# A transformer layer with 32 routed experts on one core: the last expert pair written out for TensorE in both arms of the overflow question, loaded chunk by chunk, with its down product by column halves

## What is computed

```python
logits = (ht @ w_router + b_router)            # 32 experts
top_val, top_idx = lax.top_k(logits, 4)
gates = jax.nn.softmax(top_val, axis=-1)
...
hu = xb @ w_up[e] + b_up[e]                    # 1024 -> 2048
x_glu, x_lin = jnp.split(hu, 2, axis=-1)
x_glu = jnp.minimum(x_glu, 7.0)
x_lin = jnp.clip(x_lin, -7.0, 7.0)
act = x_glu * jax.nn.sigmoid(1.702 * x_glu) * (x_lin + 1.0)
y = act @ w_down[e] + b_down[e]                # 1024 -> 1024
return y * gate[:, None].astype(y.dtype)
```

## Time and profile before

| | |
|---|---|
| median of 3 runs | 1038.88 us |
| the profiled execution, device time | 1039.46 us |
| its span in the profile | 1037.2 us |
| PE busy | 1003.5 us, 97% |
| PE weight load busy | 389.4 us, 38% |
| DVE busy | 202.7 us, 20% |
| ACT busy | 114.7 us, 11% |
| DMA, mean of the span | 410 GB/s, 423.65 MB read |
| mean granted clock of TensorE | 0.995 |

### The profile page before, as it was taken

One profiled execution on the slowest core, in us unless ns is written; L12 is line 12 of the kernel. 1 busy time (PEld: TensorE's weight loads), 2 busy tenths in 40 slices (PEclk: granted clock), 3 DMA queues, 4 the chain that ended last, 5 costly groups with the idle time before them and its releaser, 6 DMA issues.

```text
span 1037.2 us, 10934 instructions
## 1 busy us (share of the span) xinstructions
PE 1003.5 (97%) x4494; PEld 389.4 (38%) x4494; DVE 202.7 (20%) x486; ACT 114.7 (11%) x230; POOL 12.8 (1%) x26
## 2 busy tenths in 40 slices
PE   8999999999999999999999999999998989999998
PEld 4446453434343433333333333332333324232432
DVE  0466132121121121212121211212011211112012
ACT  2426111010000001010101000100001000100000
POOL 0200000000000000000000000000000000000000
PEclk9999999999999999999999999999999999999999
DMA  9955979999999999999999999999999999999996
GB/s 369 382 239 232 395 294 427 432 438 412 426 434 431 430 435 431 430 433 431 432 432 431 431 435 430 433 432 430 433 432 428 435 431 428 435 431 427 432 428 262
DMA packets 22608, 424.94 MB, mean 410 GB/s; under 512 B 3616, under 2 KB 4384, under 8 KB 6720
## 3 DMA queue, kind: packets, MB, share of 16 engines
q1 hardware_dynamic: 22208, 424.17, 96.0%
q10 hardware_dynamic: 384, 0.54, 0.2%
HBM read 423.65 MB, written 1.05 MB: 409 GB/s over the span
## 4 chain that ended last, share of the span: by engine, by line
PE 70%; DMA 28%; another core or an unknown queue 1%; DVE 0%; issue 0%; ACT 0%; POOLq 0%; SPq 0%; POOL 0%; DVEq 0%
PE psum L1424 32%; DMA everything<-in_w_moe 27%; PE psum L1458 14%; PE psum L1090 4%; PE psum L1305 4%; PE psum L1344 4%; PE psum L1214 3%; PE psum L1057 3%; PE psum L1295 2%; PE psum L1065 2%; PE psum L1082 1%; PE psum L1073 1%; PE psum L1353 0%; DMA everything<-in_x_turned 0%; PE psum L1316 0%
## 5 line engine op out<-in xcount | busy, mean ns | idle before, releaser
L1424 PE MATMUL psum<-everything 128*64 128x512 f32 x2048 | 463.7, 597 | 2.0 <-DMA everything<-in_w_moe 1.8
L1458 PE MATMUL psum<-everything 128*64 128x512 f32 x1024 | 231.3, 602 | 21.0 <-DMA everything<-in_w_moe 20.9
L1424 PEld LDWEIGHTS psum<-everything 128*64 128x64 f32 x2048 | 137.9, 136 | 295.6 <-issue 286.4
L1458 PEld LDWEIGHTS psum<-everything 128*64 128x64 f32 x1024 | 73.3, 138 | 165.7 <-issue 151.3
L736 DVE TENSOR_TENSOR everything<-psum,everything 128x512 f32<-128x512 f32 (+1 forms) x38 | 25.0, 663 | 343.2 <-PE psum L1305 332.9
L1022 DVE TENSOR_SCALAR everything<-psum 128x512 f32<-128x512 f32 x32 | 22.1, 692 | 345.0 <-PE psum L1424 345.0
L1305 PEld LDWEIGHTS psum<-everything 128*128 128x128 f32 x480 | 55.8, 191 | 24.3 <-issue 24.3
L1344 PE MATMUL psum<-everything 128*128 128x512 f32 x128 | 64.2, 606 | 0.0
L693 ACT ACTIVATE everything<-everything 128x512 f32<-128x512 f32 x32 | 20.2, 631 | 388.7 <-DVE everything L1022 388.7
L1305 PE MATMUL psum<-everything 128*128 128x128 f32 x480 | 61.5, 281 | 0.0
L1090 PE MATMUL psum<-everything 128*128 128x512 f32 x96 | 42.1, 594 | 0.0
(11 more groups left out here) (160 smaller groups left out, 300.8 us busy)
## 6 DMA issues: line engine op xcount, KB each, us to landing
everything<-in_w_moe SPq DMA_DIRECT2D x80, 4096.0 KB, 43.4
everything<-in_w_moe SPq DMA_DIRECT2D x27, 2048.0 KB, 15.1
everything<-in_w_moe SPq DMA_DIRECT2D x8, 1024.0 KB, 8.8
everything<-in_w_in SPq DMA_DIRECT2D x3, 2048.0 KB, 25.6
everything<-in_w_out SPq DMA_DIRECT2D x2, 2048.0 KB, 10.4
everything<-in_w_mem_kv SPq DMA_DIRECT2D x1, 2048.0 KB, 17.1
everything<-in_w_moe SPq DMA_DIRECT2D x4, 512.0 KB, 36.6
everything<-in_w_in SPq DMA_DIRECT2D x1, 1024.0 KB, 8.2
```

The costliest lines, as they stand in the source:

```text
L1424: mm = pe.matmul(psum[r:r + SLOTS, bank], XT[:, k, r:r + SLOTS], weights[i][:, column:column + N], start=k == 0 and not first, stop=k == K ...
L1458: mm = pe.matmul(psum[r:r + SLOTS, DOWN_BANKS[n]], actT[:, 2 * i + k, r:r + SLOTS], slot[:, column:column + N], start=i == 0 and k == 0, s ...
```

## The change

- **The last pair on TensorE is no longer in the loop.** The loop runs pairs 2 to 14. After it TensorE reads the count and branches; pair 15 is written out in full in either arm. In the arm for overflow the further blocks follow it. The other arm stands behind both in the program.
- **The last pair's loads** are issued chunk by chunk from chunk 0 (two-chunk loads are gone there), and each odd chunk has a semaphore of its own (`odd_in`), which only the written-out pair waits for. In the loop an odd chunk is covered by the wait for the even one before it, and only chunk 11 has a wait (`eleventh_in`). The increments with which SyncE kept the old semaphores level (`credit`) are gone but for one.
- **The order in a down chunk** is `n` outside and `k` inside, for every pair, and the host lays the weights out so. Half 0 is complete after two of a chunk's four groups.
- **In the last pair** combines 0 and 1 stand between the third and the fourth group of chunk 11; ScalarE copies half 1 in two pieces of 256 columns, and combine 2 is two products of 256 columns, each behind its piece. Combine 3 ends the pair.
- ScalarE's last pair is written out behind its loop.

```diff
             def pair(q, p):
                 for d in range(TWOS):
                     wait_used(q, 2 * d + 1)
                     sp.dma_start(two_slots[d], two_chunks(p * TWOS + d)).then_inc(two_in[d], 16)
-                    credit(d)
+
+                sp.sem_inc(eleventh_in, 16)
...
             def last_pair():
                 q = PAIRS - 1
-                for d in range(2):
-                    wait_used(q, 2 * d + 1)
-                    sp.dma_start(two_slots[d], two_chunks(q * TWOS + d)).then_inc(two_in[d], 16)
...
+                for j in range(PAIR_CHUNKS):
+                    wait_used(q, j)
+                    src = chunk(q * PAIR_CHUNKS + j)
+                    if j == PAIR_CHUNKS - 2:
+                        arrived = two_in[j // 2], tenth_half_in
+                    elif j == PAIR_CHUNKS - 1:
+                        arrived = quarters_in
+                    else:
+                        arrived = (odd_in if j % 2 else two_in)[j // 2],
...
-                    nc.scalar.activation(Y[:, n * N:(n + 1) * N], psum[:, DOWN_BANKS[n]], ACT.Copy).then_inc(y_ready, 1)
+                    parts = ((0, N // 2, y_half), (N // 2, N, y_ready)) if last and n == 1 else ((0, N, y_ready),)
+                    for lo, hi, ready in parts:
+                        nc.scalar.activation(Y[:, n * N + lo:n * N + hi], psum[:, DOWN_BANKS[n], lo:hi], ACT.Copy
+                                             ).then_inc(ready, 1)
...
-                    for k in range(2):
-                        if not first and i == DOWN_CHUNKS - 2 and k == 1:
-                            pe.wait_ge(tenth_half_in, q * 16)
-                        for n in range(2):
-                            if not first and last:
-                                pe.wait_ge(quarters_in[2 * k + n], q * 16)
+                    for n in range(2):
+                        if last_pair and i == DOWN_CHUNKS - 2 and n == 1:
+                            pe.wait_ge(tenth_half_in, 16)
+                        for k in range(2):
+                            if last_pair and last:
+                                pe.wait_ge(quarters_in[2 * n + k], 16)
+                                if (n, k) == (1, 1):
+                                    combine(q, (0, 1))
                             for e in range(2):
...
                 if own:
                     combine(q)
+                elif last_pair:
+                    pe.wait_ge(y_half, 1)
+                    pe.matmul(psum[:, RESULT_BANKS[2], 0:N // 2], back[:, 0], Y[:, N:N + N // 2], start=False, stop=False,
+                              skip_group_check=True)
+                    pe.wait_ge(y_ready, 2 * q + 2)
+                    pe.matmul(psum[:, RESULT_BANKS[2], N // 2:N], back[:, 0], Y[:, N + N // 2:2 * N], start=False, stop=False,
+                              skip_group_check=True).then_inc(combined, 1)
+                    combine(q, (3,))
 
             pair(0, 0, first=True)
             pair(1, 1, second=True)
-            overflow = overflowing(pe)
-            with pe.Fori(2, PAIRS) as q:
+            with pe.Fori(2, PAIRS - 1) as q:
                 pair(q, q)
-            combine(PAIRS - 1)
-            with pe.If(overflow):
+            with pe.If(overflowing(pe)):
+                pair(PAIRS - 1, PAIRS - 1, last_pair=True)
                 further_blocks(pe, lambda r, p: pair(r + PAIRS, p, own=True))
+            with pe.Else():
+                pair(PAIRS - 1, PAIRS - 1, last_pair=True)
```

More of the change, by code:

```diff
@@ L467, in pair_before_last @@
                     sp.dma_start(two_slots[d], two_chunks(q * TWOS + d)).then_inc(two_in[d], 16)
[L468 to L469 removed]
+                for j, done in ((PAIR_CHUNKS - 2, two_in[TWOS - 1]), (PAIR_CHUNKS - 1, eleventh_in)):
                     wait_used(q, j)
                     sp.dma_start(slots[j], chunk(q * PAIR_CHUNKS + j)).then_inc(done, 16)
[L472 to L473 removed]
             def last_pair():
                 q = PAIRS - 1
[L477 to L488 removed]
+                for j in range(PAIR_CHUNKS):
[7 more added lines that the diff above has]
+                        arrived = (odd_in if j % 2 else two_in)[j // 2],
+                    size = SLOT_COLS // len(arrived)
+                    for k, done in enumerate(arrived):
+                        part = slice(k * size, (k + 1) * size)
+                        sp.dma_start(slots[j][:, part], src[:, part]).then_inc(done, 16)
             def store_result():
@@ L688, in _, with pair @@
                                  ).then_inc(gatesT_ready, 1)
-            def pair(q, bdown=False):
+            def pair(q, bdown=False, last=False):
                 for i in range(2):
@@ L1363, in turn_act, with wait_chunk @@
                 mm.then_inc(act_turned, 1)
-            def wait_chunk(q, j, first):
+            def wait_chunk(q, j, first, last, own):
                 if first:
@@ L1369, in wait_chunk, with pair @@
                         pe.wait_ge(two_in[j // 2], 32)
-                    return
-                arrived = (*(two_in[j // 2] if j % 2 == 0 else None for j in range(5)), fifth_in, two_in[3], seventh_in,
-                           two_in[4], ninth_in, two_in[5], None)[j]
-                if arrived is not None:
-                    pe.wait_ge(arrived, q * 16 + 16 * (TWO_LOADS[j // 2] - 1 if j % 2 == 0 else 0))
-            def pair(q, p, first=False, second=False, own=False):
+                elif j % 2 == 0:
+                    pe.wait_ge(two_in[j // 2], q * 16 + 16 * (TWO_LOADS[j // 2] - 1))
+                elif last and j < PAIR_CHUNKS - 1:
+                    pe.wait_ge(odd_in[j // 2], 16)
+                elif not last and not own and j == PAIR_CHUNKS - 1:
+                    pe.wait_ge(eleventh_in, q * 16)
+            def pair(q, p, first=False, second=False, own=False, last_pair=False):
                 half = UP_CHUNKS // 2
```

23 lines of the change are left out of this document (10 added, 13 removed).

## The result

The changed kernel takes **1041.14 us** (median of 20 runs, 1039.31 to 1044.03), the kernel before beside it on the same chip 1038.71 (20 runs, 1037.66 to 1039.60): ratio 1.0024, 95% interval 1.0018 to 1.0030. It is 2.4 us slower where 1.4 was forecast: inside the range, but on the other side of the 0.2% line, 2.1 us. The likeliest case was the wrong one of two near ones, and the next rival, the far jump that outlasts its cover, is what happened.

What follows compares the result with a forecast made beforehand. It took the weight stream to bound the loop and TensorE, 0.8 us behind, the end; tail +0.93, output -1.6 and branch +2.1 summed to +1.4 us, 1040.3 us on the median's footing, range 1037.8 to 1043.8.

Steps and rivals of the forecast that it cites:

- 0.2% line: Whole kernel: a difference within about 0.2%, 2.1 us, counts as no change; forecast inside it, chance 0.53.
- The likeliest case: Between pairs 14 and 15: as summed, branch of 4 to 6 us with the clock up, +1.4 us; chance 0.46.
- the far jump that outlasts its cover: Rival between pairs 14 and 15: branch of 6.0 us or more makes it slower, up to +5.7 us; chance 0.42.
- What bounds the kernel: Whole kernel: weight stream bounds the loop; TensorE, 0.8 us behind it, sets the end, so lost time isn't regained.
- The branch between the pairs: TensorE, pairs 14 to 15: far branch of 5.35 us, partly covered, puts chunk 0 at 980.0, +2.1 us.
- The clock: Behind TensorE's idling before pair 15: granted clock may drop to 1.2 GHz, +1.7 us; in the 0.42 rival, not the sum.
- with the clock, 4.3 us of branch would do: Slower rival, between pairs 14 and 15: if the clock also drops, a 4.3 us branch suffices, not 6.0; chance 0.42.
- Tail: End of pair 15: combines 0 and 1 moved ahead and half 1 copied in pieces delay VectorE's last sum, +0.93 us.
- Output: Last output tile: without an instruction packet beside it, it lands at the other tiles' pace, -1.6 us.
- Loads: Last pair: chunk 0 loaded alone lands one chunk earlier, removing TensorE's 0.18 us wait and no more.
- Loop: Loop pairs: changed semaphore increments, waits and product order gain nothing, since the stream is the bound there.
- The fetch rule: TensorE's branches: a taken branch to a target outside the two pages held forces an instruction fetch before execution goes on.

Runs made afterwards that it cites:

- question_after_pair_8: Changed kernel with TensorE's count question after pair 8, both arms holding a loop of pairs 9 to 14 and pair 15: 1038.30 us, 0.9993 of the kernel before.
- one_copy: Changed kernel with pair 15 written out once behind the loop, count read after pair 1, branch at the very end: 1037.95 us, 0.9989 of the kernel before.
- arms_swapped: Changed kernel with the question reversed, so the arm that is run stands right behind the branch: 1037.69 us, 0.9991 of the kernel before.
- question_after_pair_1: Changed kernel with the question after pair 1, both arms holding a loop of pairs 2 to 14 and pair 15: 1039.51 us, 1.0008 of the kernel before.

## Why the prediction was partly right

- **What bounds the kernel.** Right: nothing after the branch gave time back, and without the stall TensorE and the stream end close together: it waits 0.17 us for the last quarter in `question_after_pair_8`, and in `one_copy` it comes to combines 0 and 1 at 1026.99, 0.95 us behind the last weight.
- **The branch between the pairs.** This step failed. Its place, its cover (3.3 us, forecast 3.2) and its packet were right. "Branch 5.35 us, chunk 0 at 980.0, +2.1" was 6.48 us in the changed kernel, and 6.09 to 6.73 in the four kernels with the question there: the idling is 1.0 us more than the sum had. The bounds of 3.35 and 9.65 held it; the value in the lower third was chosen because the packet is one and that load was 32. But most of the time is not the packet's transfer (1.07 us): it begins 4.0 us after the branch where it began 1.0 after on idle engines. That the gather started at 977.28, where "late by about 2 us, at 977" was forecast, is luck: the branch began at 970.6, 1.0 us before its forecast, and took 1.1 longer.
- **The clock.** The second part of the miss, 1.6 us in the profiled execution. It stood in the rival, not in the sum, although the sum already made TensorE idle for over 2 us and the earlier trace rows show the drop behind 1.98 us. The forecast should have carried it with a share. "In pair 15 the clock drops" was named as what would make it wrong, and it did.
- **The side of the line.** The rival's threshold, "with the clock, 4.3 us of branch would do", is not tested by a run, since every branch measured there, 6.1 to 6.7 us, lies above it and above the 6.0 without the clock. With the prediction's own sum and the two corrections, +1.4 + 1.0 + 1.6 = +4.0 where the clock falls, +2.4 where it stays up, both at or beyond 2.1.
- **Tail** +0.93: measured +0.9 in the profile, from two small errors that cancel: the combines moved ahead cost 2.08 us where 2.01 was summed, and the first half combine starts 0.46 us behind the last down product where 0.57 was. **Output** -1.6: measured -1.6 in the profile, for the reason given; by the medians roughly 1, not told from nothing. **Loads** -0.18: measured -0.23. **Loop** 0: nothing seen there, and `one_copy`, which keeps the new order and the new increments, is 0.9 us below the kernel before.
- **The fetch rule** cited from the Trainium skill was right for this place: a far target meant a packet and a stall, and in `arms_swapped`, where the branch falls through, there is neither. The same section of the Trainium skill's "Runtime: NRT & Kernel Launch" also gives TensorE's instruction memory as 128 KB, 2,048 instructions; by that figure the loop of some 530 runs without a packet, as it does, and the two pages of 256 instructions, which the prediction held against the rule, are not TensorE's. Why a leap ahead of some 1,050 needed one it doesn't say by itself.

## What to carry to other kernels

Writing a loop's last turn into both arms of a question turns a far jump at the end, where little waits for it, into one in the middle: put the arm that is run next to the question, keep one copy, or ask where the engine has several microseconds of waiting ahead of it and a deep queue of loads behind. Price a far jump by the state of the DMA engines at that moment, not by one seen at the quiet end of a program, and add the clock that the idling costs behind it. And before adding work to an engine's tail to start something sooner, compare what it adds to the path (here 2.0 us of combines and restarts) with what it takes off (1.2 us).

## What was not expected of the hardware

- A far branch costs 3.3 to 3.9 us on idle DMA engines and 6.0 to 7.9 us on full ones, seen in five and nine kernels. A packet of 16 KB (1.0 to 1.5 us of one DMA engine) lies inside each, in `question_after_pair_1` two of 1.6 and 2.2 us. The wait for it to begin, 1.0 against 3.5 to 4.5 us, makes most of the difference.
- With a single such packet in it, a 256 KB transfer spread over all engines took 1.6 to 1.7 us longer in three profiles, more than the packet's own 1.03 to 1.10 us.
- A far jump of 7.9 us at 243 us (TensorE idle for 3.9 us of it) cost the stream 2 to 3 us for good; one of 6.5 at 621 us (idle for 3.5) cost it nothing that the profile shows clearly. Each is one profile.
